# Two transformer blocks on one core: VectorE's order of work in the first layer, ten evictions on ScalarE, the recurrence's last steps inside the attention, modulation sums two panels earlier in the first feed-forward, and the last k-block of two down panels set apart

## The chip, the cores and the metric

The kernel runs on one core of a Trainium2 chip. The metric is the device time of one execution in microseconds (us); lower is better. Engines are called TensorE (PE), VectorE (DVE), ScalarE (ACT), GpSimd (POOL) and SyncE (SP, whose queue issues the loads of weights).

## The reference, cut to what matters

Two blocks of two layers each work on 512 tokens of width 1024, in float32. The change lies almost wholly in layer 0 (`layer_ab`) and in the four feed-forwards.

```python
def layer_ab(x, c, ...):
    sh_m, sc_m, g_m, sh_f, sc_f, g_f = adaln(c, mod_w, mod_b)   # silu(c) @ mod_w + mod_b, split in 6
    h = modulate(x, norm_mix, sh_m, sc_m)
    (a_gate, a_x, q, kc, vc, ks, vs, kw, vw, gts) = _split(h @ w_in, IN0_SIZES)
    y_a = rg_lru(causal_conv(a_x, conv_w, conv_b), wa, ba, wx, bx, lam) * jax.nn.gelu(a_gate)
    y_b = nsa_mixer(q, kc, vc, ks, vs, kw, vw, jax.nn.sigmoid(gts), pe_k, w1_k, w2_k, pe_v, w1_v, w2_v)
    x = x + g_m[:, None, :] * (jnp.concatenate([y_a, y_b], axis=-1) @ w_out)
    h = modulate(x, norm_ffn, sh_f, sc_f)
    return x + g_f[:, None, :] * swiglu(h, wg, wu, wd)          # (silu(h @ wg) * (h @ wu)) @ wd
```

`layer_c` (layer 1) has another attention and the same `adaln` and `swiglu`; layers 2 and 3 are the second block, whose feed-forward has a three-tap convolution on both halves before the product.

## The kernel before

Activations lie transposed: feature on the partition, 512 tokens along a row, eight k-blocks of 128 features. A **panel** is a 128x1024 piece of a weight matrix; it gives 128 output features for all tokens. There are 378 panels in one fixed sequence (`P_KC` = 0 ... `P_VW` = 17 for layer 0's input, `P_OUT0` = 18 to 25 for its output projection, `P_FFN0` = 26 onward for its feed-forward), and each goes through the same stations, in a ring of four slots (`RING`) and four PSUM banks:

- SP loads it (`load_raw`, semaphore `raw_landed`), 512 KB;
- ACT rounds it to `w_hi` (`split_hi`, `hi_ready`), which may start when PE is done with the panel four before it (`panel_done`);
- POOL takes `w_lo` = raw - `w_hi` (`split_lo`, `lo_ready`);
- PE multiplies (`panel`): three matmuls of 128x512 for each k-block, hi x hi, hi x lo, lo x hi, 24 a panel, then `panel_done`;
- DVE (or DVE and ACT together) takes the result out of the bank and gives it back (`bank_free`).

Every engine works through a program of its own in order, and waits on semaphores by hand-written counts. Nothing is scheduled by a planner.

**Modulation sums.** The modulation vectors of both layers (`adaln`) are matrix-vector products. Each **pair** of 128x1024 blocks is loaded by SP into one single buffer `modraw` (1 MB, `load_pair`), reduced over k by DVE in eight instructions (`sum_pair`, `weighted`; the semaphore `mod_summed`), and then summed over partitions by four small matmuls on PE (`mod_pair`, called by `with_mods` behind a panel; `mod_used`). `PAIR_AT` says behind which panel a pair stands: 40 pairs, at odd panels and three even ones. DVE makes the sum of the pair of panel p+2 (`AHEAD` = 2) at its own step p. SP loads the pair of panel p when two things have happened: `w_lo` of panel p is ready (`lo_ready`, since the panel's loads and the pair's stand in one queue), and the pair before is summed, which frees `modraw`:

```python
for j in range(4):
    p = P_FFN0 + j
    load_raw(it * 4 + (p + RING), (p + RING) % RING, it * 4 + (p + 1))
    if p in PAIR_AT:
        load_pair(it * 2 + PAIR_AT[p], it * 2 + summed(PAIR_AT[p] - 1))
```

**Layer 0, before the attention.** Beside the panels PE does the compression's hidden layer (`hidden`, 128 matmuls), the recurrence's gates (`lru_gates`), and the compressed attention. DVE's loop over p begins each step with `sum_mods(p + AHEAD)`, then small work that PE waits for (`turned_copies`, `diagonals`, `compressed_max`, `compressed_out`), then the bank's copy (`copy_out`), then the recurrence (`lru_conv`, `lru_scan`). After the loop come four products `ya = ya * xc` and, with ACT, their hi and lo parts; then `attention(0)`, in which all engines pass 32 pairs (i, c, branch) along: scores on PE, mask and maximum on DVE (line 1644), exponential on ACT, transposes on PE, copies on ACT and DVE, values on PE, output on DVE.

**Projection and feed-forward 0.** During the eight panels of the projection DVE makes sums, adds the result to `x`, and adds squares for the next norm; `rstd(1)` on PE then needs `acc_ready`. The feed-forward has three parts of 8, 8 and 6 columns: in each, gate and up panels alternate (`prod` = silu x up on DVE, its hi part on ACT, its lo part on DVE, `f_lo_ready`), then eight down panels contract over the part. Pairs run along until `MOD_UNTIL`, the end of the second part. In the text T is the start of a `prod` (line 1599); there are eight of them in each of the first two parts.

## Time and profile before

| what | value |
|---|---|
| median of 3 runs | 2623.41 us (2616.62 to 2627.03) |
| profiled execution, its own time | 2626.01 us |
| its span, first to last instruction | 2624.3 us |
| PE busy / DVE busy / ACT busy / POOL busy | 95% / 52% / 35% / 36% of the span |
| mean granted TensorE clock | 0.965 of 2.4 GHz |
| chain that ended last | PE 79%, issue 9%, DVE 7%, ACT 2%, POOL 2% |

The chain is the work that ended last, followed backward. It is nearly all PE, so the reading starts from the places where PE waits. Positions in time are us from the span's start.

### The profile page before, as it was taken

How to read it: one execution, taken by the hardware profiler on the slowest of the kernel's cores; microseconds unless marked ns; L12 is line 12 of the kernel's file. 1: busy time of each engine (PE TensorE's matmuls, PEld its weight loads, DVE VectorE, ACT ScalarE, POOL GpSimd, SP SyncE). 2: the span in 40 equal slices, each digit the busy share in tenths (PEclk: the TensorE clock that was granted, in tenths of full speed). 3: DMA queues.
4: the chain of work that ended last, by engine and by line, in shares of the span. 5: the costliest groups of instructions: out<-in, count | busy, mean ns of one | idle time of the engine just before them, and what ended most of it. 6: DMA issues, size and time to landing. Idle time of an engine off the chain costs nothing.

```text
span 2624.3 us, 35970 instructions
## 1 busy us (share of the span) xinstructions
PE 2482.3 (95%) x12239; PEld 2038.5 (78%) x12239; DVE 1355.9 (52%) x2511; ACT 919.0 (35%) x1466; POOL 941.4 (36%) x405
## 2 busy tenths in 40 slices
PE   8897989999999889999999969999999998999998
PEld 7676768888876667888888758888878977888886
DVE  6568665444157855111117765545456464544445
ACT  3245433222333443322234434322236363432222
POOL 2220124444443002444444624444444401344443
PEclk9998989999999889999999979999999999999998
DMA  7430135554232002322232203323232201232322
GB/s 304 176 129 33 49 129 200 187 176 174 89 104 72 25 26 79 104 96 96 96 96 97 71 27 105 104 88 104 88 112 91 95 17 33 88 104 88 104 88 72
DMA packets 64333, 263.51 MB, mean 100 GB/s; under 512 B 7264, under 2 KB 7776, under 8 KB 57952
## 3 DMA queue, kind: packets, MB, share of 16 engines
q1 hardware_dynamic: 61056, 251.00, 28.1%
q10 hardware_dynamic: 3168, 11.08, 1.1%
q8 instruction: 66, 1.08, 0.2%
q14 instruction: 43, 0.35, 0.0%
HBM read 259.95 MB, written 2.10 MB: 100 GB/s over the span
## 4 chain that ended last, share of the span: by engine, by line
PE 79%; issue 9%; DVE 7%; ACT 2%; POOL 2%; DVEq 1%; DMA 1%; POOLq 0%; ACTq 0%; SPq 0%
PE bank L593 23%; PE bank L595 23%; PE bank L594 22%; PE bank L767 4%; PE bank L745 3%; PE bank L755 2%; POOL w_lo L564 1%; DVE bank L2093 1%; DMA modraw<-in_pairs 1%; DVE acc L1462 1%; DVE bank L1736 1%; PE bank L779 1%; PE bank L696 0%; DVE iacc L2026 0%; DVE cval L1579 0%
## 5 line engine op out<-in xcount | busy, mean ns | idle before, releaser
L564 POOL TENSOR_TENSOR w_lo<-raw,w_hi 128x1024 fp32r<-128x1024 f32 x378 | 911.3, 2418 | 1654.4 <-ACT w_hi L1098 1653.4
L593 PE MATMUL bank<-h_hi,w_hi 128*128 128x512 f32 x1760 | 702.7, 399 | 29.2 <-DVE h_lo L1509 7.8
L594 PE MATMUL bank<-h_lo,w_hi 128*128 128x512 f32 x1760 | 693.9, 394 | 0.0
L595 PE MATMUL bank<-h_hi,w_lo 128*128 128x512 f32 x1760 | 693.5, 394 | 0.0
L1098 ACT ACTIVATE w_hi<-raw 128x1024 fp32r<-128x1024 f32 x378 | 393.6, 1052 | 536.0 <-PE bank L595 533.2
L593 PE MATMUL bank<-g_hi,w_hi 128*128 128x512 f32 x1072 | 420.5, 392 | 7.2 <-DVE g_lo L1614 5.6
L593 PEld LDWEIGHTS bank<-h_hi,w_hi 128*128 128x128 f32 x1760 | 336.1, 191 | 111.2 <-issue 12.4
L595 PE MATMUL bank<-g_hi,w_lo 128*128 128x512 f32 x1072 | 418.5, 390 | 0.0
L594 PE MATMUL bank<-g_lo,w_hi 128*128 128x512 f32 x1072 | 418.3, 390 | 0.0
L595 PEld LDWEIGHTS bank<-h_hi,w_lo 128*128 128x128 f32 x1760 | 335.7, 191 | 72.2
L594 PEld LDWEIGHTS bank<-h_lo,w_hi 128*128 128x128 f32 x1760 | 336.6, 191 | 69.3 <-issue 0.5
L593 PEld LDWEIGHTS bank<-g_hi,w_hi 128*128 128x128 f32 x1072 | 202.2, 189 | 50.2 <-DVE g_lo L1614 6.8
L595 PEld LDWEIGHTS bank<-g_hi,w_lo 128*128 128x128 f32 x1072 | 201.9, 188 | 42.6
L594 PEld LDWEIGHTS bank<-g_lo,w_hi 128*128 128x128 f32 x1072 | 202.2, 189 | 41.8
L1599 DVE TENSOR_TENSOR prod<-silu,bank 128x512 f32<-128x512 f32 x44 | 30.3, 688 | 304.2 <-PE bank L595 304.0
L1163 ACT ACTIVATE g_hi<-prod 128x512 f32 x66 | 41.7, 632 | 300.8 <-DVE prod L1599 197.8
L1525 DVE SCALAR_TENSOR_TENSOR x<-bank,plain,x 128x512 f32<-128x512 f32 x64 | 48.0, 750 | 185.3 <-PE bank L595 185.3
L1736 DVE SCALAR_TENSOR_TENSOR bank<-modraw,csil,bank 128x256 f32<-128x256 f32 x240 | 117.3, 489 | 17.9
L1203 ACT ACTIVATE prob<-prob,stat 128x512 f32<-128x512 f32 (+1 forms) x192 | 105.5, 552 | 22.8 <-DVE stat L1644 22.5
L1525 DVE SCALAR_TENSOR_TENSOR x<-bank,modv,x 128x512 f32<-128x512 f32 x64 | 47.8, 749 | 106.2 <-PE bank L595 104.5
L1644 DVE CUSTOM_DVE_ANT_0 prob<-bank,mask 128x512 f32<-128x512 f32 (+1 forms) x192 | 86.5, 488 | 25.5 <-PE bank L745 21.7
L1573 DVE TENSOR_TENSOR bank<-bank,rb 128x512 f32<-128x512 f32 x88 | 61.4, 698 | 64.9 <-PE bank L595 53.7
(294 smaller groups left out, 2656.1 us busy)
## 6 DMA issues: line engine op xcount, KB each, us to landing
raw<-in_panels SPq DMA_DIRECT2D x378, 512.0 KB, 3.3
modraw<-in_pairs SPq DMA_DIRECT2D x40, 1024.0 KB, 5.5
first_mods<-in_first SPq DMA_DIRECT2D x4, 2048.0 KB, 21.1
w<-in_w ACTq DMA_DIRECT2D x2, 2048.0 KB, 9.0
x<-in_x SPq DMA_DIRECT2D x1, 2048.0 KB, 7.9
out<-yout ACTq DMA_DIRECT2D x8, 256.0 KB, 2.1
mask<-in_causal ACTq DMA_DIRECT2D x1, 1024.0 KB, 4.9
mask<-in_dilated ACTq DMA_DIRECT2D x1, 1024.0 KB, 4.9
```

The source lines that it names most:

```text
L564: pool.tensor_tensor(w_lo[:, slot, :], raw[:, slot, :], w_hi[:, slot, :].bitcast(F32), ALU.subtract)\
L593: pe.matmul(out, w_h, m_h, start=start, stop=False)
L594: pe.matmul(out, w_h, m_l, start=False, stop=False)
L595: return pe.matmul(out, w_l, m_h, start=False, stop=stop)
L745: pe.matmul(bank[SBANK[(2 * n + b) % 3]][:, 0:w], q_of(run, pairs_[n], b), k_of(run, pairs_[n], b), start=True, stop=True).then_inc(score_ ...
L767: m = pe.matmul(bank[4 + n % 2][:, HD * b:HD * b + HD], probT[:, 2 * (n % 2) + b, P * j:P * j + P], v_of(run, pairs_[n], b, j), start=(j = ...
L1098: act.activation(w_hi[:, slot, :], raw[:, slot, :], ACT.Copy).then_inc(hi_ready, 1)
L1203: act.activation(row, row, ACT.Exp, bias=stat[:, 0, u % 64:u % 64 + 1], scale=-1.0, accum_out=stat[:, 1, u % 64:u % 64 + 1]).then_inc(exp_ ...
L1525: dve.scalar_tensor_tensor(out=x[:, n, :], in0=bank[p % RING][:, :], scalar=scale_by, in1=x[:, n, :], op0=MUL, op1=ADD).then_inc(bank_free, 1)
L1573: dve.tensor_tensor(bank[slot][:, :], bank[slot][:, :], rb[:, :], MUL)
L1644: dve.tensor_tensor_reduce(prob[:, 2 * (n % 2) + b, 0:w], bank[SBANK[(2 * n + b) % 3]][:, 0:w], mask[:, i, 0:w], -SCALE, HIGHEST, ADD, ALU ...
L1736: m = dve.scalar_tensor_tensor(out=part if k < KB - 1 else to, in0=w[:, :, k, :], scalar=csil[:, k:k + 1], in1=part, op0=MUL, op1=ADD)
```

## The change

Five things are altered:

1. In DVE's loop of layer 0 the small work that PE waits for comes ahead of `sum_mods`; the gates' split moves from step 4 to 2; `lru_scan(3)` moves from step 17 to 16. On PE `hidden(0)` comes ahead of the pair behind panel 3.
2. ACT copies the banks of ten panels (q, the gate branch, ks, kw) that DVE copied.
3. The recurrence's products for chunks 2 and 3 come in step 16; those of 0 and 1, and all hi and lo parts, move into `attention(0)`: products at n = 2, 3, hi parts on ACT at n = 5 to 8, lo parts on DVE at n = 8 to 11.
4. `PAIR_AT` puts one pair behind panel `P_AGATE` (10) and none behind `P_OUT0 + 6`. In feed-forward 0 DVE makes the sum of the pair four panels on (`2 * AHEAD`) instead of two, and a second sum stands ahead of the first `prod`.
5. `two_first`: in every feed-forward's part the first two down panels do all k-blocks but the last, one after the other, and then both last ones.

```diff
-    if _p % 2 or _p in (P_OUT0 + 2, P_OUT0 + 4, P_OUT0 + 6):
+    if _p % 2 or _p in (P_AGATE, P_OUT0 + 2, P_OUT0 + 4):
...
+            def two_first(p, m_hi, m_lo, size, f):
+
+                for ks in (range(size - 1), range(size - 1, size)):
+                    for q in (p, p + 1):
+                        at = q % RING
+                        if ks[0] == 0:
+                            pe.wait_ge(lo_ready, q + 1)
+                            pe.wait_ge(bank_free, q - RING + 1)
+                        for k in ks:
+                            pe.wait_ge(f_lo_ready, f + k + 1)
+                            m = three(bank[at][:, :], w_hi[:, at, P * k:P * k + P], w_lo[:, at, P * k:P * k + P],
+                                      m_hi[:, k, :], m_lo[:, k, :], k == 0, k == size - 1)
+                        if ks[0]:
+                            m.then_inc(panel_done, 1)
...
-                    panels(p, KB, *down, size, moving=(f_lo_ready, f), mods=p < MOD_UNTIL)
+                    two_first(p, *down, size, f)
+                    panels(p + 2, KB - 2, *down, size, mods=p < MOD_UNTIL)
...
                 panel(p, p % RING, h_hi, h_lo)
-                with_mods(p)
                 if p == 3:
                     hidden(0)
-                elif p == 4:
+                with_mods(p)
+                if p == 4:
...
+                def recurrence_high(c):
+
+                    act.wait_ge(y_ready, c + 1)
+                    of = (2, 3, 0, 1)[c]
+                    act.activation(h_hi[:, of, :], ya[:, of, :], ACT.Copy).then_inc(y_hi, 1)
...
+                    if run == 0 and n in (5, 6, 7, 8):
+                        recurrence_high(n - 5)
...
+                if P_Q0 <= p < P_VS:
+                    copy_out(p)
                 split_hi(p + RING)
             act.wait_ge(panel_done, P_OUT0)
-            for c in range(LC):
-                act.wait_ge(y_ready, c + 1)
-                act.activation(h_hi[:, c, :], ya[:, c, :], ACT.Copy).then_inc(y_hi, 1)
             attention(0)
...
                             if p < MOD_UNTIL:
-                                m = PAIR_AT[pu + AHEAD]
+                                m = PAIR_AT[pu + 2 * AHEAD]
                                 sum_pair(m, it * 32 + 16 * (m + 1), it * 2 + (summed(m) - 2))
...
-                            sum_mods(p + n + AHEAD)
+                            sum_mods(p + n + 2 * AHEAD)
                             add_x(p + n, n, out_gate(layer, True, n))
...
+                    if run == 0 and n in (2, 3):
+                        recurrence_gated(n - 2)
+                    elif run == 0 and n in (8, 9, 10, 11):
+                        recurrence_low(n - 8)
...
             norm_h(1)
             sum_mods(P_FFN0 + 1)
+            sum_mods(P_FFN0 + 3)
             ffn(0, P_FFN0, 1)
```

DVE at step 11 of layer 0. Before, after the scan of the recurrence's chunk 0 (`inp`, `xc`), the eight instructions of a modulation sum (`modraw`, `modsum`) stand ahead of the compressed scores' mask and maximum (`cprob`), which PE waits for:

```order
L1858 SCALAR_TENSOR_TENSOR xc<-decay,inp 128x512
L1731 TENSOR_SCALAR bank<-modraw,csil 128x256
L1736 SCALAR_TENSOR_TENSOR bank<-modraw,csil,bank 128x256 x6
L1736 SCALAR_TENSOR_TENSOR modsum<-modraw,csil,bank 128x256
L1901 TENSOR_TENSOR cprob<-bank,cmask 128x256 x4
```

and now:

```order
L1903 SCALAR_TENSOR_TENSOR xc<-decay,inp 128x512
L1958 TENSOR_TENSOR cprob<-bank,cmask 128x256 x4
L1964 TENSOR_REDUCE cst<-cprob 128x32
L1967 TENSOR_SCALAR cst<-cst 128x32
L1969 TENSOR_TENSOR cprob<-cprob,cst 128x1024
L1776 TENSOR_SCALAR bank<-modraw,csil 128x256
L1781 SCALAR_TENSOR_TENSOR bank<-modraw,csil,bank 128x256 x6
L1781 SCALAR_TENSOR_TENSOR modsum<-modraw,csil,bank 128x256
```

The sum has moved behind the compressed scores' four instructions.

DVE from the values' copy (`vtok`) to the first masked scores of the attention (`prob`). Before, behind the copy come the last scan, the four products (`ya`) and the four lo parts (`h_lo`):

```order
L1736 SCALAR_TENSOR_TENSOR modsum<-modraw,csil,bank 128x256
L1449 COPY vtok_111<-bank 128x512 x2
L1849 TENSOR_TENSOR inp<-inp,xc 128x512
L1850 MEMSET axp 128x1
L1852 TENSOR_TENSOR inp<-inp,axp 128x512
L1855 SCALAR_TENSOR_TENSOR inp<-decay,inp 128x511
L1858 SCALAR_TENSOR_TENSOR xc<-decay,inp 128x512
L1990 TENSOR_TENSOR ya<-ya,xc 128x512 x4
L1993 TENSOR_TENSOR h_lo<-ya,h_hi 128x512 x4
L1716 TENSOR_TENSOR modv<-bank,cols 128x18
L1644 ISA prob,stat<-bank,mask 128x512
```

and now:

```order
L1900 SCALAR_TENSOR_TENSOR inp<-decay,inp 128x511
L1903 SCALAR_TENSOR_TENSOR xc<-decay,inp 128x512
L1909 TENSOR_TENSOR ya<-ya,xc 128x512 x2
L1776 TENSOR_SCALAR bank<-modraw,csil 128x256
L1781 SCALAR_TENSOR_TENSOR bank<-modraw,csil,bank 128x256 x6
L1781 SCALAR_TENSOR_TENSOR modsum<-modraw,csil,bank 128x256
L1490 COPY vtok_111<-bank 128x512 x2
L1761 TENSOR_TENSOR modv<-bank,cols 128x20
L1685 ISA prob,stat<-bank,mask 128x512
```

The last scan and two products now stand ahead of the sum and the copy, and only the small `modv` lies between the copy and the first scores.

DVE from the end of layer 0's second norm (`h_lo`) to the first product of feed-forward 0 (`prod`). Before, one sum lies between them:

```order
L1509 SCALAR_TENSOR_TENSOR h_lo<-tn,modv,h_hi 128x512 x2
L1731 TENSOR_SCALAR bank<-modraw,csil 128x256
L1736 SCALAR_TENSOR_TENSOR bank<-modraw,csil,bank 128x256 x6
L1736 SCALAR_TENSOR_TENSOR modsum<-modraw,csil,bank 128x256
L1593 UNCONDITIONAL_BRANCH
L1593 ISA
L1598 ISA
L1599 TENSOR_TENSOR prod<-silu,bank 128x512
```

and now:

```order
L1550 SCALAR_TENSOR_TENSOR h_lo<-tn,modv,h_hi 128x512 x2
L1776 TENSOR_SCALAR bank<-modraw,csil 128x256
L1781 SCALAR_TENSOR_TENSOR bank<-modraw,csil,bank 128x256 x6
L1781 SCALAR_TENSOR_TENSOR modsum<-modraw,csil,bank 128x256
L1776 TENSOR_SCALAR bank<-modraw,csil 128x256
L1781 SCALAR_TENSOR_TENSOR bank<-modraw,csil,bank 128x256 x6
L1781 SCALAR_TENSOR_TENSOR modsum<-modraw,csil,bank 128x256
L1634 UNCONDITIONAL_BRANCH
```

A second sum, of the pair of panel `P_FFN0 + 3`, has come in ahead of the loop. Inside the loop the order of kinds is as before; the pair that is summed behind a product is now that of four panels on. SP's order of loads is unchanged.

## Rows read from the trace of the kernel before

**Rows 1.** The page, section 1: busy us (share of the span) x instructions.
```profile
PE 2482.3 (95%) x12239; PEld 2038.5 (78%) x12239; DVE 1355.9 (52%) x2511; ACT 919.0 (35%) x1466; POOL 941.4 (36%) x405
```

**Rows 2.** What PE waited for, 56 to 222 us: us, times, longest.
```profile
PE bank L745 <- DVE stat L1644: 13.3, 1, 13.3
PE bank L614 <- DVE modsum L1736: 5.7, 2, 5.3
PE bank L820 <- DVE cprob L1901: 2.9, 1, 2.9
```

**Rows 3.** PE's timeline: start, us, instruction, count [idle before <- releaser].
```profile
74.48 10.11 PE L831 MATMUL bank<-w,blocks 64*32 64x128 f32 x128 [1.83 <-DVE blocks L1866]
...
109.11 7.07 PE L831 MATMUL bank<-w,blocks 64*32 64x128 f32 x126
...
154.91 3.01 PE L820 MATMUL bank<-xc,lruw 64*64 64x512 f32 x8 [2.89 <-DVE cprob L1901]
...
164.06 1.93 PE L820 MATMUL bank<-xc,lruw 64*64 64x512 f32 x8
```

**Rows 4.** DVE's timeline ahead of the attention.
```profile
189.33 0.69 DVE L1849 TENSOR_TENSOR inp<-inp,xc 128x512 f32<-128x512 f32 x1
...
191.65 1.23 DVE L1858 TENSOR_TENSOR_SCAN xc<-decay,inp 128x512 f32<-128x512 f32 x1
...
201.44 2.71 DVE L1849 TENSOR_TENSOR inp<-inp,xc 128x512 f32<-128x512 f32 x1
...
215.07 0.69 DVE L1644 CUSTOM_DVE_ANT_0 prob<-bank,mask 128x512 f32<-128x512 f32 x1
```

**Rows 5.** Busy us by engine (PE, PEld, DVE, ACT, POOL), PEclk, DMA share, GB/s.
```profile
225.00:235.00 10.00, 10.00 (x78) 7.97 (x76) 7.96 (x36) 6.32 (x22) 0.00 (x0) 1.00 0.00 0
...
304.00:330.00 26.00, 25.23 (x107) 20.82 (x108) 15.32 (x30) 4.54 (x6) 7.21 (x3) 0.90 0.37 127
```

**Rows 6.** PE's timeline at the projection's end.
```profile
356.85 0.89 PE L614 MATMUL bank<-ones,modsum 128*128 128x1 f32 x4 [3.13 <-DVE modsum L1736]
...
362.99 1.87 PE L683 MATMUL bank<-ones,acc 128*128 128x1 f32 x8 [5.24 <-DVEq L1465]
```

**Rows 7.** DVE's timeline in the projection: a sum starts, ends, the next one starts.
```profile
343.08 0.49 DVE L1731 TENSOR_SCALAR bank<-modraw,csil 128x256 f32<-128x256 f32 x1 [3.44 <-DMA modraw<-in_pairs]
...
347.66 0.69 DVE L1462 TENSOR_TENSOR acc<-acc,sq 128x512 f32<-128x512 f32 x1 [0.16 <-issue]
...
352.37 0.49 DVE L1731 TENSOR_SCALAR bank<-modraw,csil 128x256 f32<-128x256 f32 x1 [3.36 <-DMA modraw<-in_pairs]
...
361.17 1.72 DVE L1462 TENSOR_TENSOR acc<-acc,sq 128x512 f32<-128x512 f32 x1 [0.76 <-ACT sq L1108]
```

**Rows 8.** DVE's timeline in feed-forward 0.
```profile
382.91 0.49 DVE L1731 TENSOR_SCALAR bank<-modraw,csil 128x256 f32<-128x256 f32 x1
...
390.55 0.69 DVE L1599 TENSOR_TENSOR prod<-silu,bank 128x512 f32<-128x512 f32 x1 [3.21 <-PE bank L595]
...
421.93 0.69 DVE L1599 TENSOR_TENSOR prod<-silu,bank 128x512 f32<-128x512 f32 x1 [3.56 <-PE bank L595]
...
467.48 0.69 DVE L1599 TENSOR_TENSOR prod<-silu,bank 128x512 f32<-128x512 f32 x1 [4.68 <-PE bank L595]
...
524.41 0.69 DVE L1599 TENSOR_TENSOR prod<-silu,bank 128x512 f32<-128x512 f32 x1 [7.50 <-PE bank L595]
```

**Rows 9.** POOL's timeline behind the product at 421.93.
```profile
424.41 2.39 POOL L564 TENSOR_TENSOR w_lo<-raw,w_hi 128x1024 fp32r<-128x1024 f32 x1 [3.90 <-ACT w_hi L1098]
```

**Rows 10.** SP's queue: a panel's load and a pair's, one behind the other.
```profile
175.33 0.33 SPq L520 DMA_DIRECT2D raw<-in_panels  x1
175.71 0.43 SPq L526 DMA_DIRECT2D modraw<-in_pairs  x1
```

**Rows 11.** DVE's timeline: the sum that waited for that pair.
```profile
181.26 0.49 DVE L1731 TENSOR_SCALAR bank<-modraw,csil 128x256 f32<-128x256 f32 x1 [2.13 <-DMA modraw<-in_pairs]
```

**Rows 12.** Who waited for `prod`'s lo parts (line 1614), whole kernel: us, times.
```profile
  PE bank L593: 11.1, 6
```

More of the change, by code:

```diff
@@ L672, in panels @@
                     panel(p, p % RING, m_hi, m_lo, nk)
+                    if mods:
+                        with_mods(p)
[12 more added lines that the diff above has]
+                            m.then_inc(panel_done, 1)
+                if p < MOD_UNTIL:
+                    with_mods(p + 1)
             def with_mods(p):
@@ L906, in _ @@
                     pe.wait_ge(cmp_ready, 1)
+                    pe.wait_ge(bank_free, P_AGATE)
                     compressed_scores()
@@ L1234, in _, with copy_out @@
             act.dma_start(cmask[:, :, :], A["cmask"]).then_inc(masks_landed, 16)
+            def copy_out(p):
+                act.wait_ge(panel_done, p + 1)
+                if p == P_Q0:
+                    act.wait_ge(bank_free, P_Q0)
+                if p < P_AGATE:
+                    out = q0[:, p - P_Q0, :]
+                elif p < P_KS:
+                    out = ya[:, p - P_AGATE, :]
+                else:
+                    out = (ksT if p == P_KS else kwT)[:, :]
+                act.activation(out, bank[p % RING][:, :], ACT.Copy).then_inc(bank_free, 1)
             def hidden_gelu(kv):
@@ L1858, in lru_scan, with recurrence_gated, recurrence_low @@
                 dve.tensor_tensor_scan(xc[:, c, :], a, inp[:, c, :], 0.0, MUL, ADD).then_inc(scanned, 1)
+            def recurrence_gated(c):
+                dve.wait_ge(agelu_ready, c + 1)
+                dve.drain()
+                dve.tensor_tensor(ya[:, c, :], ya[:, c, :], xc[:, c, :], MUL).then_inc(y_ready, 1)
+            def recurrence_low(c):
+                dve.wait_ge(y_hi, c + 1)
+                of = (2, 3, 0, 1)[c]
+                dve.tensor_tensor(h_lo[:, of, :], ya[:, of, :], h_hi[:, of, :].bitcast(F32), SUB).then_inc(y_lo, 1)
             def lay_blocks(kv, src):
@@ L1940, in _ @@
             for p in range(P_OUT0):
-                sum_mods(p + AHEAD)
-                if p == 9:
+                if p == P_VC:
+                    copy_out(p, vcT[:, :])
+                    dve.wait_ge(w1_landed, 48)
+                    dve.drain()
+                    lay_blocks(0, kcT)
+                    lay_blocks(1, vcT)
+                elif p == 2:
+                    dve.wait_ge(gate_split, 1)
+                    dve.tensor_tensor(wg_lo[:, :, :], w_small[:, :, :], wg_hi[:, :, :].bitcast(F32), SUB).then_inc(gate_split, 1)
+                elif p == 9:
                     turned_copies()
@@ L1955, in _ @@
                     compressed_out(3)
-                if p in (P_KC, P_VC, P_KS, P_KW):
-                    copy_out(p, {P_KC: kcT, P_VC: vcT, P_KS: ksT, P_KW: kwT}[p][:, :])
-                elif p < P_Q0:
+                sum_mods(p + AHEAD)
+                if p == P_KC:
+                    copy_out(p, kcT[:, :])
+                elif P_AX <= p < P_Q0:
                     copy_out(p, axp[:, p - P_AX, TAPS_LRU - 1:])
-                elif p < P_AGATE:
-                    copy_out(p, q0[:, p - P_Q0, :])
-                elif p < P_KS:
-                    copy_out(p, ya[:, p - P_AGATE, :])
+                    lru_conv(p - P_AX)
                 elif p == P_VW:
+                    dve.wait_ge(bank_free, P_VS)
                     copy_tokens(P_VS, vtok0, 0)
-                if p == P_VC:
-                    dve.wait_ge(w1_landed, 48)
-                    dve.drain()
-                    lay_blocks(0, kcT)
-                    lay_blocks(1, vcT)
-                elif P_AX <= p < P_Q0:
-                    lru_conv(p - P_AX)
                 if p == 3:
@@ L1984, in _ @@
                     lru_scan(2)
-                elif p == 17:
                     lru_scan(3)
-            for c in range(LC):
-                dve.wait_ge(agelu_ready, c + 1)
-                dve.drain()
-                dve.tensor_tensor(ya[:, c, :], ya[:, c, :], xc[:, c, :], MUL).then_inc(y_ready, 1)
-            for c in range(LC):
-                dve.wait_ge(y_hi, c + 1)
-                dve.tensor_tensor(h_lo[:, c, :], ya[:, c, :], h_hi[:, c, :].bitcast(F32), SUB).then_inc(y_lo, 1)
+                    recurrence_gated(2)
+                    recurrence_gated(3)
             dve.wait_ge(masks_landed, 32)
```

4 lines of the change are left out of this document (1 added, 3 removed).

## The prediction

> **What bounds the kernel now.** I read the page first: PE is busy for 95% of the span [rows 1], and the chain is mostly PE. So time can be won only where PE waits, and any new wait of PE, or any stretch in which another engine becomes slower than PE, is paid in full. Then I read PE's waits by stage. Ahead of the attention there are three of some length: 13.3 us for the first masked scores, 5.3 for the modulation sum behind panel 3, 2.9 for the compressed scores [rows 2]. In the projection's end PE waits 3.1 and 5.2 us [rows 6]. In feed-forward 0 it hardly waits: a product starts each (467.48 - 421.93) / 4 = 11.39 us [rows 8], which is two panels and one pair on PE. Last I read what DVE does in each of these places, and for feed-forward 0 the whole loop of product, split, load and sum, since the change moves the sum in it.
>
> **Part 1, layer 0 up to the attention.** The sum behind panel 3 and the blocks for `hidden(0)` cost 5.3 and 1.8 us of waiting [rows 2, 3]. With `hidden` ahead of the pair and the blocks laid ahead of the sum, both go: the sum still has the 7 us of `hidden` to be made. The first `hidden` also took 10.11 us where the second took 7.07 for 126 of its 128 matmuls [rows 3]; the first stands right behind two waits, the second behind none. I count 2.9 us of that. At step 11 the wait of 2.9 goes, and the gates behind it took 3.01 us instead of 1.93 [rows 3]: 1.1. The first matmuls of the panels behind both places lose about 1 more, an estimate by the same ratio. In all PE comes to the end of the token panels 15 us sooner.
>
> There DVE decides. Its step 16 began its scan at 189.33 [rows 4]; 15 us sooner that is 174.3. Behind it now stand two scans of 3.6 us each (189.33 to 191.65 + 1.23 [rows 4]), 2 us for one instruction that is slow beside POOL, as the one at 201.44 was (2.71 instead of 0.69 [rows 4]), two products (1.6 with their drains), the sum (4.4, below), the values' copy and `modv` (1.7). That gives 191.2 for the first masked scores, against 215.07 [rows 4]: **-24 us**. It would be -15 if both scans went at the slow pace and the pair of panel 19 came late, -28 if PE's end decided.
>
> ACT's ten copies: ACT is busy 35% [rows 1] and stands four panels ahead of PE with `w_hi`. A copy of this size costs DVE or ACT about 0.7 us, as `prod` does [rows 8]; one lies ahead of each split, and a split has the three other panels in the ring as cover. I take nothing; without that cover it would be 10 x 0.7 = 7.
>
> **Part 2, in the attention.** DVE gets two products and four lo parts, six instructions of 0.78 us with a drain. In a stretch of 10 us, which is four pairs, it is busy 7.96 [rows 5], so 0.51 is free in each pair, and PE is busy all the time. 6 x (0.78 - 0.51) = **+1.5 us**; nothing at best, 4.7 if no slack is usable. ACT's four hi parts fit in its 0.92 free a pair [rows 5].
>
> **Part 3, the projection.** DVE is bound there by sum and load in turn, since `modraw` is a single buffer: 343.08 to 352.37 is 9.29 us for one pair, 4.42 of it the sum and 4.87 the load [rows 7]. One pair fewer lets DVE come to its last square, and so to `acc`, 9.3 us sooner. PE then goes on at once from the last panel: 3.13 + 5.24 + the small pair's 0.4 = 8.8 us [rows 6]. The three groups of small matmuls up to the norm's factors run behind these waits at about 1.87 us each [rows 6]; with the ratio seen at the gates, 3.01 to 1.93 [rows 3], they lose 0.6 each to the clock, and I add 1.7. **-10.5 us**, between -8 and -12.
>
> **Part 4, feed-forward 0.** This is the large term. Follow one product at T = 421.93 [rows 8]. ACT makes its hi part, then `w_hi` of the panel four on; POOL's `w_lo` of that panel ends at 424.41 + 2.39 = T + 4.9 [rows 9]. Only then may SP issue the pair that belongs to that panel, because `load_pair` stands in the queue behind `lo_ready` of the same panel. Before, DVE asked behind this product for the pair of two panels on, whose load had been allowed one turn earlier. Now it asks for the pair of four panels on, which at this moment isn't issued. The load of a panel goes out first and the pair's 0.38 behind it; from the first of these issues to the sum's start it was 181.26 - 175.33 = 5.9 us [rows 10, 11]. So the sum starts at T + 4.9 + 0.2 + 5.9 = T + 11.0, ends 4.4 later, and with the drain the next product starts at T + 15.7. DVE does nothing in the load's time, and the next product waits behind the sum in DVE's program; its hi part opens the next load. It is a loop, and it has no slack that could run out: 15.7 us against 11.39.
>
> The first product: two sums now stand ahead. The first starts at 382.91 [rows 8]; with its sum and the next load (9.3), the second sum (4.4) and 0.2, the first product starts at 396.8 instead of 390.55 [rows 8]. Seven turns later the eighth starts at 396.8 + 7 x 15.7 = 506.7 instead of 467.48: +39.2. (All these in the old run's time, without the gain of parts 1 to 3.) The second part adds 7 x 4.3 = +30.2.
>
> The down panels between. From the eighth product to the next part's first it was 524.41 - 467.48 = 56.9 us [rows 8]. `two_first` helps: PE has done 14 of 16 k-blocks of two panels when the last lo part comes, and both are ready about 7 us sooner. But the sum behind the eighth product ends at T + 15.6, the next pair is loaded behind it and is summed by about T + 25.5, and the `add_x` that gives back the second down bank stands behind that sum. PE would want this bank at about T + 22: 4 to 5 us of waiting. I take +1 for the first stretch and -2 for the second, whose end no product follows that a sum delays, and +2 for a lower clock behind these waits. **+70 us** for the feed-forward. At the loads' fastest (4.9 alone [rows 7], issued with nothing beside) a turn is 15.1 and the sum +60; with a load 1 us slower it is +84.
>
> **Part 5, `two_first` in the other feed-forwards.** PE waited for lo parts of products six times, 11.1 us in all [rows 12]. The cover for the last k-block doubles from 5 or 7 k-blocks to 10 or 14. **-11 us**, at worst 0.
>
> **The sum** against the profiled execution's 2626.0 us: -24 + 1.5 - 10.5 + 70 - 11 = +26, so 2652. That execution lies 2.6 above the median of the three runs shown, 2623.4; against the median I forecast **2650 us**, 1.0% slower. With the bounds together in either direction, not all at once, this case lies between 2634 and 2672.
>
> **The clock.** PE now idles about 4.3 us in each turn. In the stretch 304 to 330 the granted clock was 0.90 of 2.4 GHz behind the attention's end [rows 5]; at 1.2 GHz for the missing part that is 26 x 0.10 = 2.6 us of work lost. 11.4 + 2.6 = 14.0 still fits in a turn of 15.7, so I add nothing in the turns. The Trainium skill ("TensorE: Matmul & The Clock Gate", HAM oscillation) says that a wait for a load in every turn of a loop can throw the clock down anew each time. By that rule alone the cost would come 14 times; the second rival below says where it would bite.
>
> **Rivals.**
> - *The loop is not closed (faster).* If the sum's data were there by T + 6.7 (11.39 - 4.42 - 0.3), PE would stay the bound, part 4 would be nought, and the rest gives 2650 - 70 = **2580**. For it: before the change DVE sat idle 3 to 5 us in each turn [rows 8], so there seems to be room, and the pair's load is 4.9 us. Against it: `w_lo` of the panel that gates the load ends at T + 4.9 [rows 9] already, and the load can't be done 1.8 us later. 12%.
> - *The clock falls for good in the turns (much slower).* If both panels of a turn ran at 1.2 GHz throughout, a turn would take PE 22.8 us: 14 x 7.1 = 99 more, **2750**. Against it: PE works over 11 us in each turn, and in the stretch above it had its full clock back within a part of that. The rule of the Trainium skill named above would make this more likely. 4%.
> - *Losses small, gains large (no change).* Turns of 15.1 and a first layer at its best: +60 - 28 - 12 - 12 = +8, **2631**. 8%.
> - The case forecast: 76%.
>
> **Chances.** About 0.5%, 13 us, is what a measurement of this kernel tells from no change, so the border of slower is 2636.5. Slower: the forecast case but for its lower edge (0.05), and the clock: 0.75. Within: the third rival and that edge: 0.13. Faster: 0.12. The range 2622 to 2676 holds the forecast case and the third rival and leaves out the first two.
>
> **What would show it.** First masked scores of the attention near 191 us instead of 215; PE's `column_sums` about 31 us sooner than 362.99. In feed-forward 0 the products 15 to 16 us apart, each sum's first instruction waiting 5 to 6 us for `modraw`, PE waiting on line 614 or for its bank in every turn, PE's busy share falling to about three quarters from 360 to 470 and again in the second part. In layers 2 and 3 no waits for lo parts of products. The prediction is wrong if products stay 11.4 apart: then a pair's load was issued ahead of `w_lo` of its panel, and I misread the queue.

## The result, and the profile after

| | before | after |
|---|---|---|
| median, runs taken side by side on one chip | 2620.01 us (2615.99 to 2627.03) | 2671.3 us (2665.53 to 2674.31) |
| profiled execution, its own time / span | 2626.01 / 2624.3 us | 2665.53 / 2663.7 us |
| mean granted TensorE clock | 0.965 | 0.962 |

The ratio is 1.0181, with a 95% interval of 1.0163 to 1.0198: slower, by 1.8%. The forecast was 2650. The two spans differ by 39.4 us, the two medians by 51. The profiled execution of before lies 6 us above its median in this comparison, and that of after 6 us below; the positions below are from the two profiled executions and add up to the 39.4 (the last row's 39.8 less 0.4 behind it). So the table explains 39.4 of the 51. The rest can't be placed; executions of one kernel spread by as much, of which more under the experiments.

| place (us from the start) | before | after | difference | change since the row above | forecast of that |
|---|---|---|---|---|---|
| first masked score of attention 0 | 215.1 | 196.2 | -18.9 | -18.9 | -24 |
| its last masked score | 294.0 | 277.1 | -16.9 | +2.0 | +1.5 |
| `column_sums`, end of the projection | 363.0 | 336.5 | -26.5 | -9.6 | -10.5 |
| first product of feed-forward 0 | 390.5 | 371.2 | -19.3 | +7.2 | +6.3 |
| its eighth product | 467.5 | 487.7 | +20.2 | +39.5 | +33 |
| first product of the second part | 524.4 | 549.5 | +25.1 | +4.8 | +1 |
| its eighth | 604.1 | 664.5 | +60.3 | +35.3 | +30.2 |
| `column_sums` behind feed-forward 0 | 748.3 | 807.6 | +59.4 | -1.0 | -2 (+2 for the clock) |
| `column_sums` behind attention 1 | 1026.1 | 1079.8 | +53.7 | -5.7 | 0 |
| end of feed-forward 1 | 1408.2 | 1467.3 | +59.1 | +5.4 | part 5: |
| end of feed-forward 2 | 1969.3 | 2018.0 | +48.7 | -10.4 | -11 in all |
| end of feed-forward 3 | 2610.4 | 2650.2 | +39.8 | -8.9 | |

The page's busy shares and chain, after (engine, busy us, share of the span, instructions; then shares of the chain):

```profile
PE 2495.6 (94%) x12239; PEld 2045.6 (77%) x12239; DVE 1356.8 (51%) x2501; ACT 921.6 (35%) x1476; POOL 946.3 (36%) x405
...
PE 64%; issue 23%; POOL 5%; DVE 5%; ACT 1%; DVEq 1%; DMA 0%; POOLq 0%; SPq 0%; ACTq 0%
```

PE's busy share fell from 95% to 94% [rows 1] only, since the loss is in a tenth of the span. The chain shows it better: PE's part of it fell from 79% to 64%.

PE's waits after, from the end of the projection to the end of feed-forward 0 (who waits, for what, us in total, times, longest):

```profile
PE bank L614 <- DVE modsum L1781: 33.1, 12, 4.4
PE bank L593 <- DVE g_lo L1655: 12.1, 2, 6.2
PE bank L593 <- DVE x L1566: 6.2, 2, 3.3
```

None of these three is there before in more than 2.0 us. A turn is the time from one product of feed-forward 0 to the next. One of them, on DVE's timeline after (start us, duration us, engine, line, operation, tiles, count, and in brackets the idle time ahead of it and what released it):

```profile
388.61 0.69 DVE L1640 TENSOR_TENSOR prod<-silu,bank 128x512 f32<-128x512 f32 x1 [0.25 <-issue]
390.21 0.69 DVE L1655 TENSOR_TENSOR g_lo<-prod,g_hi 128x512 f32 x1 [0.92 <-ACT g_hi L1184]
399.60 0.49 DVE L1776 TENSOR_SCALAR bank<-modraw,csil 128x256 f32<-128x256 f32 x1 [8.70 <-DMA modraw<-in_pairs]
400.16 3.30 DVE L1781 SCALAR_TENSOR_TENSOR bank<-modraw,csil,bank 128x256 f32<-128x256 f32 x6
403.61 0.48 DVE L1781 SCALAR_TENSOR_TENSOR modsum<-modraw,csil,bank 128x256 f32<-128x256 f32 x1
404.72 0.69 DVE L1640 TENSOR_TENSOR prod<-silu,bank 128x512 f32<-128x512 f32 x1 [0.63 <-issue]
```

and what opens it, on POOL's and on SP's timeline in the same turn:

```profile
391.08 2.38 POOL L564 TENSOR_TENSOR w_lo<-raw,w_hi 128x1024 fp32r<-128x1024 f32 x1 [12.55 <-ACT w_hi L1119]
```

```profile
393.67 0.33 SPq L520 DMA_DIRECT2D raw<-in_panels  x1
394.39 0.33 SPq L526 DMA_DIRECT2D modraw<-in_pairs  x1
```

The product starts at 388.61; `w_lo` of the panel four on ends at 393.46, SP issues that panel's next load at 393.67 and the pair at 394.39. DVE has nothing to do for 8.70 us, sums from 399.60, and the next product follows the sum at 404.72: 16.1 us for this turn where it was 11.39 [rows 8]. It is the loop of the forecast, link by link. The bracket of the last row says "issue": the product waited for nothing but DVE's own program.

Ahead of the attention, DVE's and POOL's timelines after, where the compression's blocks are laid:

```profile
62.84 4.56 DVE L1923 TENSOR_TENSOR blocks<-kcT,peT 128x496 f32<-128x496 f32 x2 [1.50 <-DMA w<-in_w]
67.32 5.99 DVE L1923 TENSOR_TENSOR blocks<-vcT,peT 128x496 f32<-128x496 f32 x2
...
77.16 0.48 DVE L1781 SCALAR_TENSOR_TENSOR modsum<-modraw,csil,bank 128x256 f32<-128x256 f32 x1
```

```profile
61.17 11.35 POOL L564 TENSOR_TENSOR w_lo<-raw,w_hi 128x1024 fp32r<-128x1024 f32 x4 [15.87 <-ACT w_hi L1119]
```

Each pair of block instructions had taken 1.87 us before. Here they took 10.5 us in all (62.84 to 73.31), beside four `w_lo`. So the sum behind `hidden` ended at 77.6, too late for PE. PE's waits up to 222 us, after:

```profile
PE bank L765 <- DVE vtok L1490: 5.1, 1, 5.1
PE bank L614 <- DVE modsum L1781: 3.0, 1, 3.0
...
PE bank L851 <- DVE blocks L1923: 0.3, 1, 0.3
```

The 13.3 us for the masked scores (`stat`) [rows 2] have become 0.8, but PE now waits 5.1 for the values' copy (`vtok`) ahead of them, where it waited 1.0 before. The 5.3 for the sum behind panel 3 [rows 2, 3] have become 3.0. DVE is done with `modv` at 194.1 and then waits for PE's scores itself:

```profile
196.20 0.69 DVE L1685 CUSTOM_DVE_ANT_0 prob<-bank,mask 128x512 f32<-128x512 f32 x1 [2.08 <-PE bank L765]
```

### The profile page after: what moved, and what is told of

Read it like the earlier page. It is cut to its first block, busy times and chain, and to the rows that moved or that the text cites. A ratio compares the mean times of both kernels' runs of the same rounds, so it can differ in the third digit from the quotient of the medians.

```text
span 2663.7 us, 35805 instructions
## 1 busy us (share of the span) xinstructions
PE 2495.6 (94%) x12239; PEld 2045.6 (77%) x12239; DVE 1356.8 (51%) x2501; ACT 921.6 (35%) x1476; POOL 946.3 (36%) x405
## 4 chain that ended last, share of the span: by engine, by line
PE 64%; issue 23%; POOL 5%; DVE 5%; ACT 1%; DVEq 1%; DMA 0%; POOLq 0%; SPq 0%; ACTq 0%
PE bank L593 19%; PE bank L595 19%; PE bank L594 19%; POOL w_lo L564 5%; PE bank L787 2%; PE bank L775 1%; PE bank L765 1%; DVE bank L2142 1%; DVE acc L1503 1%; PE bank L799 0%; PE bank L715 0%; DMA modraw<-in_pairs 0%; DVE iacc L2075 0%; DVE x L1566 0%; DVE h_lo L1587 0%
## 5 line engine op out<-in xcount | busy, mean ns | idle before, releaser
L593 PE MATMUL bank<-g_hi,w_hi 128*128 128x512 f32 x1072 | 423.2, 395 | 21.4 <-DVE g_lo L1655 12.1
L593 PEld LDWEIGHTS bank<-h_hi,w_hi 128*128 128x128 f32 x1760 | 339.8, 193 | 113.9 <-issue 11.4
L1776 DVE TENSOR_SCALAR bank<-modraw,csil 128x256 f32<-128x256 f32 x40 | 19.4, 486 | 205.8 <-DMA modraw<-in_pairs 205.4
```

Source lines behind the costliest of these rows:

```text
L593: pe.matmul(out, w_h, m_h, start=start, stop=False)
```

## The experiments

My theory: all of the loss is the sums' move in feed-forward 0, through the pair's late load, and the rest of the change is a gain of about 40 us. The rivals: TensorE's clock in the turns, or DVE's own longer order of work, costs it; or the other parts don't gain. The kernel before ran again beside each group: 2624.4 us (2616.1 to 2629.2), 2624.8 and 2621.9. Where the kernels compared differ by less than 10 us, I go by positions in the traces as well, since the runs of one kernel spread by up to 15 us.

This spread goes with the mean granted clock of the execution. The four runs of e1 (below) took 2580.5, 2581.5 and 2583.4 us at 0.974, 0.973 and 0.973, and 2591.3 at 0.969. That last one was profiled, and its trace shows where the time lies: layer 2's attention took 193.6 us at 0.89 and layer 3's 282.2 at 0.96, from `column_sums` to `column_sums`, where the changed kernel took 189.8 at 0.92 and 276.7 at 0.98 for the same work. So medians of kernels that differ by less than 10 us are also set by how many of their runs had the lower clock; I compare those at the same clock. Why an execution has the one or the other is open.

**e1: all of the change but the sums' move.**

```diff
-                                m = PAIR_AT[pu + 2 * AHEAD]
+                                m = PAIR_AT[pu + AHEAD]
...
-                            sum_mods(p + n + 2 * AHEAD)
+                            sum_mods(p + n + AHEAD)
...
             sum_mods(P_FFN0 + 1)
-            sum_mods(P_FFN0 + 3)
```

> The changed kernel with one thing undone: in feed-forward 0 the sum is again that of the pair two panels on, and no second sum stands ahead of the first product. Loop theory (the load of the pair four panels on can only be issued behind the product that asks for its sum): products 11.4 us apart again, and all of the 86 us that the changed kernel lost between 363 us of before and the second norm come back; against before it is faster by the gain ahead of the feed-forward (26.5 at column_sums) and by what two_first gives in layers 2 and 3 (16 in the trace of the changed kernel), less about 5 in feed-forward 1: 2620 - 37 = 2583 us. Rival (two_first delays what ACT and SP do for the down panels, and the loss is its own): products may be 11.4 apart but the stretch from an eighth product to the next first one stays near 62 us, and the time stays above 2610.

Measured: 2582.47 us (2580.46 to 2591.28), ratio 0.9846 [0.9820, 0.9872]. From the third on the products are 11.4 us apart again, and from the first one to the end of feed-forward 0 every place stands 24.7 us ahead of the kernel before.

**e2: the sums' move alone, on the kernel before.** The same lines the other way round.

> The kernel before with one thing of the change alone: sums four panels on in feed-forward 0, and the second sum ahead of the first product. Loop theory: products 16.5 us apart as in the changed kernel, first product 7 us later, and 75 to 85 us more in all than before, so 2695 to 2705; without two_first PE waits in the first down panel for the last lo part, some 6 us more a part. Rival (the loss needs the other parts, such as the extra pair or two_first): under 40 us more.

Measured: 2707.72 us (2704.44 to 2711.63), ratio 1.0324 [1.0294, 1.0353]. The first product is 7.1 us late, the eighth 51.7, the second part's first 57.3, its eighth 93.0; the end of feed-forward 0 is 93.1 late. PE's waits there:

```profile
PE bank L614 <- DVE modsum L1736: 38.9, 12, 5.3
PE bank L593 <- DVE g_lo L1614: 20.9, 2, 11.3
```

The move alone costs 83 us by the medians; beside the rest of the change it costs 2671.3 - 2582.5 = 89. By the positions at the end of feed-forward 0 it is the other way round: 93.1 alone, and 807.6 - 723.6 = 84.1 beside the rest. The positions fit the second row: PE waited 20.9 us for lo parts here and 12.1 with `two_first`, which is nearly the 9.0 between them. Behind feed-forward 0, e2 gets 8.6 of its 93.1 back, 4.6 of them in attention 1.

**e3: the whole change, with each pair's load issued two panels sooner.** SP issues the pair of panel p+2 where it issued that of p, so that the load no longer stands behind `w_lo` of its own panel.

```diff
+            load_pair(PAIR_AT[P_FFN0 + 1], summed(PAIR_AT[P_FFN0 + 1] - 1))
...
                     if p in PAIR_AT:
-                        load_pair(it * 2 + PAIR_AT[p], it * 2 + summed(PAIR_AT[p] - 1))
+                        m = PAIR_AT[p + 2]
+                        load_pair(it * 2 + m, it * 2 + summed(m - 1))
```

> The changed kernel, sums still four panels on, but in feed-forward 0 SP issues each pair's load two panels sooner in its queue (the pair of panel p + 2 at panel p), so that it waits only for the sum that frees the buffer and for the split of a panel that was made a turn ago. Nothing else is changed. Loop theory: the gate is what closes the loop; a turn falls from 16.5 to PE's 11.4, DVE no longer waits for modraw behind a product, and the time is that of the kernel with the sums two panels on but for the second sum ahead of the first product, 2583 + 0 to 7. Rival (one buffer is too few for sums four panels on, whatever the queue: load and sum, 9.3 us, must follow one another behind each product): turns of 14 us or more remain and the time stays above 2620.

Measured: 2585.02 us (2583.55 to 2587.65), ratio 0.9862 [0.9836, 0.9888]. On DVE's timeline a turn now reads:

```profile
374.04 0.69 DVE L1646 TENSOR_TENSOR prod<-silu,bank 128x512 f32<-128x512 f32 x1 [0.42 <-issue]
375.66 0.69 DVE L1661 TENSOR_TENSOR g_lo<-prod,g_hi 128x512 f32 x1 [0.93 <-ACT g_hi L1190]
378.98 0.49 DVE L1782 TENSOR_SCALAR bank<-modraw,csil 128x256 f32<-128x256 f32 x1 [2.62 <-DMA modraw<-in_pairs]
...
383.75 0.69 DVE L1646 TENSOR_TENSOR prod<-silu,bank 128x512 f32<-128x512 f32 x1 [0.25 <-issue]
```

and on SP's:

```profile
374.18 0.34 SPq L526 DMA_DIRECT2D modraw<-in_pairs  x1
...
383.68 0.33 SPq L526 DMA_DIRECT2D modraw<-in_pairs  x1
```

The load starts right behind the sum that frees `modraw`, the wait shrinks from 8.70 to 2.62 us, and a turn of 9.7 is open to DVE. Its first product is 8 us later than e1's, since the second sum still stands ahead of it, but by the eighth that is made up (-24.5 against -24.7). So neither DVE's order of work nor the number of sums ahead costs anything in the turns: what costs is the place of the pair's load in SP's queue, alone.

**e4: `two_first` alone, in all four feed-forwards, on the kernel before.** The diff's lines for `two_first` and its call.

> The kernel before with two_first alone, in all four feed-forwards. In the changed kernel's trace feed-forwards 2 and 3 were 8 us each faster and feed-forward 1 was 5 slower, with two new waits of 2.2 and 1.8 at its end. If two_first is the cause of both: 2620 - 11 = 2609, waits for products' lo parts gone in layers 2 and 3, and the end of feed-forward 1 later by 4 to 5. If the loss in feed-forward 1 comes from elsewhere (timing of loads shifted by the rest of the change): 2604 and no wait for the folded lo parts at panel P_AG.

Measured: 2610.03 us (2606.73 to 2615.48), ratio 0.9952 [0.9939, 0.9965]. Feed-forward 0 keeps its length, feed-forwards 2 and 3 are 8.0 and 7.9 us shorter, and feed-forward 1 is 5.3 us longer. PE's new waits in feed-forward 1, where before there was one of 0.2 us for `h_lo` of this line:

```profile
PE bank L593 <- DVE h_lo L1566: 2.2, 1, 2.2
PE bank L593 <- POOL w_lo L564: 1.8, 1, 1.8
```

DVE's timeline over the last eight down panels of feed-forward 1, first in e4, then the first column and the last one in the kernel before:

```profile
1372.19 0.75 DVE L1545 SCALAR_TENSOR_TENSOR x<-bank,modv,x 128x512 f32<-128x512 f32 x1 [5.15 <-PE bank L595]
...
1378.90 3.71 DVE L1482 TENSOR_TENSOR acc<-acc,sq 128x512 f32<-128x512 f32 x2
1382.53 0.74 DVE L1545 SCALAR_TENSOR_TENSOR x<-bank,modv,x 128x512 f32<-128x512 f32 x1
...
1407.10 0.75 DVE L1545 SCALAR_TENSOR_TENSOR x<-bank,modv,x 128x512 f32<-128x512 f32 x1
...
1410.06 3.65 DVE L1482 TENSOR_TENSOR acc<-acc,sq 128x512 f32<-128x512 f32 x2
```

```profile
1368.07 0.75 DVE L1525 SCALAR_TENSOR_TENSOR x<-bank,modv,x 128x512 f32<-128x512 f32 x1 [1.76 <-PE bank L595]
...
1404.08 0.74 DVE L1525 SCALAR_TENSOR_TENSOR x<-bank,modv,x 128x512 f32<-128x512 f32 x1
...
1406.52 1.48 DVE L1462 TENSOR_TENSOR acc<-acc,sq 128x512 f32<-128x512 f32 x2
```

Here, as not in feed-forwards 2 and 3, DVE also makes `h_lo` and adds squares for each column, and from the second column on it never waits for PE: 1382.53 to 1392.90 is 10.4 us for two columns, where PE's two panels of six k-blocks take 8.1 (before, the second column came 4.07 us behind the first, as PE gave it). So DVE is the slower of the two. `two_first` brings the first column 4.1 us later than before, 0.7 of it from before this place. DVE makes up a part, and the last column starts 3.0 us later (1407.10 against 1404.08). Its additions of squares end at 1413.7 instead of 1408.0, which is 5.7: the other 2.7 us are the last column's own, with additions of 3.65 us instead of 1.48 and an `h_lo` of 1.27 instead of 0.75. In both kernels every second column is slow in this way, each time with a whole `w_lo` beside it; with the delay the last column has become one of these. So about half of the 5.3 us is the late first column and half is what the last one fell beside.

**e5: the first layer's changes alone** (e1 without `two_first`).

> The changed kernel with the sums again two panels ahead and with the down panels in their old order everywhere: parts 1 to 3 of the change alone. Parts add: two_first alone gave 2624.4 - 2610.0 = 14.4, all but the sums' move gave 2582.5, so this kernel should give 2582.5 + 14.4 = 2597 (2592 to 2602), ratio 0.990, with column_sums near 338.5 and every later place 24 to 25 us ahead of the kernel before. If the two parts share a gain (both shorten the same wait of TensorE in feed-forward 0), it is below 2590; if they work against each other, above 2602.

Measured: 2592.58 us (2590.32 to 2596.43), ratio 0.9881 [0.9866, 0.9897]. In the trace the projection ends 24.9 us sooner than before, and 25.4 stay to the end of feed-forward 0. `two_first` on top of it gives 10.1 by the medians. In the traces it gives 6.4 and 6.5 us in feed-forwards 2 and 3 and takes 5.3 in feed-forward 1, which is 7.7 of the 10.1; the rest isn't placed.

**e6: e1 with `two_first` in layers 2 and 3 only.**

```diff
-                    two_first(p, *down, size, f)
-                    panels(p + 2, KB - 2, *down, size, mods=p < MOD_UNTIL)
+                    if layer >= 2:
+                        two_first(p, *down, size, f)
+                        panels(p + 2, KB - 2, *down, size)
+                    else:
+                        panels(p, KB, *down, size, moving=(f_lo_ready, f), mods=p < MOD_UNTIL)
```

> The kernel of the first experiment (sums two panels ahead), with two_first in layers 2 and 3 only. If two_first costs 5.3 us in feed-forward 1 because new waits arise at its end, and does nothing in feed-forward 0, then 2582.5 - 5 = 2577 (2574 to 2580), ratio 0.982, and feed-forward 1 as long as in the kernel before. If the 5.3 us were a variation between executions, 2582.5, ratio 0.984.

Measured: 2579.0 us (2577.87 to 2593.31), ratio 0.9839 [0.9817, 0.9862]. In the trace feed-forward 1 is 5.2 us shorter than in e1, and the span is 2576.5. By the times e1 and e6 can't be told apart; by the place where they differ they can. By its median e6 is the fastest kernel of the study, 1.6% ahead of the kernel before and 3.5% ahead of the changed one.

**e7: e1 with the pair of panel 10 back behind the projection's seventh panel.**

```diff
-    if _p % 2 or _p in (P_AGATE, P_OUT0 + 2, P_OUT0 + 4):
+    if _p % 2 or _p in (P_OUT0 + 2, P_OUT0 + 4, P_OUT0 + 6):
```

> The kernel of the first experiment, with the pair of panel 10 moved back behind the seventh panel of the projection. Part 3's reason (VectorE is bound by sum and load in turn in the projection, 9.3 us a pair): column_sums comes 8 to 10 us later than in the first experiment and stays so, 2582.5 + 8 = 2591, with the first masked score up to 1 us sooner, as step 8 has one sum fewer. Rival: the gain of the projection came from the earlier entry into it and not from the pair: then the same time as the first experiment, 2582.

Measured: 2589.58 us (2588.66 to 2596.53), ratio 0.9875 [0.9860, 0.9891]. The first masked score comes 1.7 us sooner, and `column_sums` 7.8 us later than in e1. Its waits in the projection:

```profile
PE bank L702 <- DVEq L1506: 5.5, 1, 5.5
PE bank L799 <- DVE h_lo L1729: 3.1, 3, 1.0
PE bank L614 <- DVE modsum L1781: 2.3, 1, 2.3
```

The two waits of part 3 [rows 6], the first and the third line, are back with the pair; e1 has neither of them in this stretch.

**e8: e1 with the ten evictions on VectorE again.**

> The kernel of the first experiment, with the ten evictions on VectorE again, each behind the step's sum as before the change. If VectorE is what sets the first masked score, ten copies of 0.7 us come back on its path: first masked score 4 to 7 us later, 2582.5 + 5 = 2588. If the copies lie in VectorE's waits for loads and panels, which come at every step, only those of steps 14 to 16 count: 0 to 2 us, 2583.

Measured: 2589.5 us (2581.63 to 2591.9), ratio 0.9870 [0.9855, 0.9885]. In the trace the first masked score is 1.1 us sooner than in e1, and `column_sums` too. The medians lie 7 us apart the other way, but that is the clock: e8's run at 0.973 took 2581.6 us, as e1's two at 0.973 did (2581.5 and 2583.4), and its other three, at 0.969 and 0.970, took 2589.2 to 2591.9, as e1's at 0.969 did (2591.3). The copies' move gives nothing that these runs can tell.

**e9: e1 with the recurrence's products, hi and lo parts ahead of the attention again.**

> The kernel of the first experiment, with the recurrence's four products and its hi and lo parts ahead of the attention again. If VectorE's work between its last scan and the first masked score is what PE waits for, two products more (1.6 us) and the chain of hi and lo parts (ScalarE's last hi part and VectorE's last lo part behind it, some 3 us) come on the path: first masked score 4 to 6 us later, and the attention, which has six VectorE instructions fewer, 1.5 to 2 us shorter; together +3, 2585.5. If the move does nothing because the attention's start waits on something else, the first masked score stays and the time is 2580.5.

Measured: 2592.71 us (2584.95 to 2594.07), ratio 0.9889 [0.9873, 0.9906]. The first masked score is 3.5 us later, the attention 2.3 shorter, `column_sums` 1.4 later. On DVE's timeline:

```profile
193.90 4.92 DVE L2040 TENSOR_TENSOR ya<-ya,xc 128x512 f32<-128x512 f32 x4
198.74 2.49 DVE L2043 TENSOR_TENSOR h_lo<-ya,h_hi 128x512 fp32r<-128x512 f32 x4
```

PE's waits up to 222 us now have 6.3 us for the masked scores and 3.5 for `vtok`, where e1 has 0.8 and 5.1. The move is worth 1.4 us by positions. The medians say more (10), but three of e9's four runs had a clock of 0.967 or 0.968, which none of e1's had; its profiled one, at 0.972, took 2584.95, 1.5 to 4.5 us above e1's three at 0.973 and 0.974.

**e10: e1 with the blocks laid behind the modulation sum again.**

```diff
                 if p == P_VC:
                     copy_out(p, vcT[:, :])
-                    dve.wait_ge(w1_landed, 48)
-                    dve.drain()
-                    lay_blocks(0, kcT)
-                    lay_blocks(1, vcT)
...
                 sum_mods(p + AHEAD)
+                if p == P_VC:
+                    dve.wait_ge(w1_landed, 48)
+                    dve.drain()
+                    lay_blocks(0, kcT)
+                    lay_blocks(1, vcT)
```

> The kernel of the first experiment, with the compression's blocks laid behind the modulation sum again, as before the change, but hidden still ahead of the pair on TensorE. In the first experiment the four block instructions took 10.4 us beside GpSimd's w_lo, where they had taken 3.7 before, and the four w_lo took 11.4 instead of 9.5. If it is GpSimd working at the same time that stretches them, the blocks take 3.7 us again here, after 71.7, and TensorE waits 4 to 6 us for the first of them instead of 3.0 for the sum behind hidden: 0 to 3 us slower, 2584. If the blocks are slow by themselves in this place (their inputs just written), they take 10 us here too, TensorE waits 8 us, and the time is 2588.

Measured: 2588.99 us (2585.55 to 2599.0), ratio 0.9886 [0.9863, 0.9910]. DVE's and POOL's timelines:

```profile
68.57 3.30 DVE L1781 SCALAR_TENSOR_TENSOR bank<-modraw,csil,bank 128x256 f32<-128x256 f32 x6
...
72.58 1.88 DVE L1923 TENSOR_TENSOR blocks<-kcT,peT 128x496 f32<-128x496 f32 x2 [0.16 <-issue]
74.38 1.89 DVE L1923 TENSOR_TENSOR blocks<-vcT,peT 128x496 f32<-128x496 f32 x2
```

```profile
60.64 7.09 POOL L564 TENSOR_TENSOR w_lo<-raw,w_hi 128x1024 fp32r<-128x1024 f32 x3 [15.09 <-ACT w_hi L1119]
68.04 2.34 POOL L564 TENSOR_TENSOR w_lo<-raw,w_hi 128x1024 fp32r<-128x1024 f32 x1 [0.30 <-ACT w_hi L1119]
```

The same four instructions take 3.7 us (72.58 to 76.27) when POOL is idle, so their 10.5 us are POOL's doing. The rival, that they are slow because their inputs were just written, isn't tested by this run, where the copies lie 11 us back; but in the kernel before `vcT` was copied right ahead of them (71.67), POOL was idle, and they took 3.7 too. They still start too late here: PE waits 7.8 us for the first of them, against 0.3 + 3.0, and `column_sums` is 3.2 us later than in e1. Laying them first, slow as they are, is the better order.

## Why the prediction came out as it did

The side was right, and so was the step that decided it, but the size was about half: +26 was forecast, and measured are +39.4 between the profiled executions and +51 between the medians. The forecast lay 13.5 us under the profiled execution (2652 against 2665.5), and 21 under the median, near the upper end of its range. Some luck is in that too: the parts that were forecast were put 23 us too low in sum, and 9.0 us that nobody forecast, in the three attentions behind feed-forward 0, went the other way.

**Part 4, the loop: right in mechanism, 16 us too small in size.** From `column_sums` to `column_sums` it cost 85.9 us against 70. The turn was put at 15.7 us and measured 16.64 on average over the first seven. Its three links, mean of those seven: product to the pair's issue 5.71 (forecast 5.5), issue to the sum's start 6.02, between 5.21 and 7.50 (forecast 5.5), sum to the next product 4.91 (forecast 4.7). The load is the largest error: I had priced it from one row, and in the turns it varies. Over the fourteen turns that is 6.5 + 5.1 = 11.6 us. One sign was misread: each sum's first instruction was to wait 5 to 6 us for `modraw`, and DVE sat idle 8.7 to 10.9 there, since it is idle from its lo part on, before the load is even issued. The stretch of down panels was put at +1 and cost +4.8 (e2: +5.6). The prediction worked out a wait of 4 to 5 us for the second bank there; PE waited 3.3. That isn't what cost the time: PE was done with the up panel of the next part's first product 56.0 us after the eighth (the pair behind it starts at 543.50), where before it came after 56.9. DVE held the product 5.8 us longer:

```profile
543.47 0.49 DVE L1776 TENSOR_SCALAR bank<-modraw,csil 128x256 f32<-128x256 f32 x1 [5.37 <-DMA modraw<-in_pairs]
...
547.99 0.75 DVE L1566 SCALAR_TENSOR_TENSOR x<-bank,modv,x 128x512 f32<-128x512 f32 x1
549.47 0.69 DVE L1640 TENSOR_TENSOR prod<-silu,bank 128x512 f32<-128x512 f32 x1 [0.73 <-issue]
```

The sum ahead of it waits for its load as in a turn. The loop doesn't end with the turns; it goes on through the down panels, where I had let `two_first` make up for it.

**Part 1: the mechanism right in the main, -18.9 against -24.** Two steps were off. The first is "with `hidden` ahead of the pair and the blocks laid ahead of the sum, both go". It costed the blocks at the pace of the row before, 1.87 us a pair of instructions, although in their new place they run beside `w_lo`. The prediction knew the effect (it allowed 2 us for one slow scan instruction, and one there took 2.21), but did not ask it of the instructions that it moved. Of 10.0 us of waits that were to go (5.3 + 1.8 + 2.9), 3.3 stayed, and the scan of step 16 began at 177.98 rather than 174.3: 3.7 us. The second is the end of the path. The prediction let the first masked scores follow `modv` at once, but PE's own scores come behind the values' copy, and DVE waited 2.08 us for them (the row at 196.20 above): a term that was put at nothing. Between the two DVE was 0.8 us quicker than forecast. The gain of the slow clock behind these waits came as forecast: `hidden(0)` took 7.18 us instead of 10.11 [rows 3].

**Part 2: right** (+2.0 against +1.5; e9, which takes these instructions out again, -2.3).

**Part 3: right** (-9.6 against -10.5). e7 measures the pair's place by itself at 7.8, where the chain of sum and load said 9.3. (The sign "`column_sums` about 31 us sooner" doesn't follow from the parts, which give -24 + 1.5 - 10.5 = -33; it came 26.5 sooner.)

**ACT's copies at nothing: right** (e8).

**Part 5: the sum right, its terms not.** -11 was forecast, -8.0 and -7.9 in feed-forwards 2 and 3 and +5.4 in feed-forward 1 are -10.5. The count of waits for lo parts [rows 12] gave the gains too small, since the clock falls behind such waits: in e4 the waits of 5.5 us for `h_lo` in feed-forward 2 went, and 8.0 us with them, 2.5 of these off PE's busy time. And "at worst 0" was wrong: a later first column costs where DVE has no slack behind it, and the rows of feed-forward 1's down panels, on which that could be read, were not read.

**The clock in the turns: right to add nothing.** The granted clock was 0.86 from 371 to 488 us after, where it was 1.00 in the turns before. PE's timeline after, at the end of one of its waits:

```profile
388.51 1.01 PE L614 MATMUL bank<-ones,modsum 128*128 128x1 f32 x4 [3.68 <-DVE modsum L1781]
389.39 0.80 PE L593 MATMUL bank<-h_hi,w_hi 128*128 128x512 f32 x1
389.99 0.63 PE L594 MATMUL bank<-h_lo,w_hi 128*128 128x512 f32 x1
```

A matmul takes 0.63 us there instead of 0.39, the lower of the clock's two levels; such a stretch, of some 3 to 6 us, came in five of the first six turns. The Trainium skill ("TensorE: Matmul & The Clock Gate", HAM oscillation) says that a wait in every turn can throw the clock down each time, and this trace nearly agrees. But no product waited for it, since the panels were done within the turn: the rival of 22.8 us a turn did not come, and e3, which took away only the load's delay, took away all of the cost.

**Outside the forecast:** attention 1, which the change does not touch, took 92.2 us instead of 98.9. Windows over it, before and after (us, busy time and instructions of each engine, granted clock, DMA):

```profile
865.00:967.00 102.00, 91.80 (x598) 70.38 (x598) 76.50 (x293) 52.42 (x163) 0.38 (x1) 0.87 0.02 6
```

```profile
925.00:1021.00 96.00, 85.05 (x602) 65.01 (x602) 76.77 (x293) 52.88 (x164) 0.66 (x1) 0.95 0.02 7
```

The work is the same and the clock is 0.95 instead of 0.87. In e4, which leaves layer 0 alone, it was as long as before (99.1 us); in e2 it was 6 us shorter, and in the other experiments it took 92.2 to 95.1. So it seems to go with the kernel, though each kernel has one trace only; by what, stays open. The stretches of the attentions of layers 2 and 3 were 2.3 and 1.0 us shorter as well.

## What to carry to other kernels

When a consumer in a software pipeline is moved further ahead, move its load's place in the queue by as much: a load that stands behind a semaphore of its own turn closes a loop with the consumer, and its whole latency is then paid in each turn, however idle the engines look. Find such a loop by following one item from the moment its buffer is freed to the moment it is asked for. And price a moved instruction by who works beside it in its new place, and a delayed result by how full the engine that consumes it is up to the stage's end, not by their rows of before.

## What the runs showed of the hardware that was not expected

DVE's `TENSOR_TENSOR` with both inputs in SBUF is slowed by POOL's `w_lo`, and slows it: four instructions of 128x496 took 10.5 us (after) and 3.7 us (e10, POOL idle), and four `w_lo` beside them took 11.35 us, 2.84 each against 2.39 [rows 9] elsewhere. DVE's sum instructions, which accumulate in a PSUM bank, were not slowed beside a `w_lo`: six took 3.30 us in e10 while POOL worked from 68.04 to 70.38, as everywhere. The Trainium skill ("SBUF — State Buffer", SBUF: two separate sides) says that a DVE instruction with two SBUF inputs and a GpSimd instruction that reads SBUF exclude each other on a shared pair of ports. Both halves of these numbers agree with it in kind: the blocks have two such inputs, the sums have one there and one in PSUM. In size they fall a little short of full exclusion, by which the eight instructions would take 4 x 2.39 + 3.7 = 13.3 us one after the other; they took 12.1 (61.17 to 73.31).
